# Long convolution of the first block: PE taps, norm and silu by tokens

## The reference, cut to what matters

```python
ya = a_val * jax.nn.sigmoid(a_gate)                      # 256 tokens x 512 channels
ya = causal_dwconv(ya, w_dw_a[l], b_dw_a[l])             # 31 taps, one weight per channel and tap
ya = jax.nn.silu(layer_norm(ya, ln_a_g[l], ln_a_b[l]))   # mean and variance over the 512 channels of a token
ya = ya @ w_pw_a[l]                                      # 512 -> 1024
...
merged = jax.nn.sigmoid(gate_a) * ya + jax.nn.sigmoid(gate_b) * yb
mix = merged @ w_out[l]
```

## Time and profile before

| | us |
|---|---|
| median of 3 runs | 1148.27 |
| lowest and highest | 1147.22, 1149.77 |
| the profiled execution, its own time | 1147.8 |
| its span in the profile | 1145.8 |
| busy: PE, PE weight loads | 1088.8, 1021.4 |
| busy: DVE, ACT, POOL | 798.3, 597.4, 3.3 |

### The profile page before, as it was taken

How to read it: one execution, slowest core, us unless ns; L and a number is a source line. 1 busy time by engine, 2 the same in 40 slices (tenths; PEclk the granted TensorE clock), 3 DMA queues, 4 the chain that set the end, 5 groups by cost and what they waited for, 6 DMA issues and landing times.

```text
span 1145.8 us, 19024 instructions
## 1 busy us (share of the span) xinstructions
PE 1088.8 (95%) x7792; PEld 1021.4 (89%) x7792; DVE 798.3 (70%) x1375; ACT 597.4 (52%) x1004; POOL 3.3 (0%) x13
## 2 busy tenths in 40 slices
PE   7998989999999999979989999999999899999997
PEld 7998879899999988779988799999899787999996
DVE  7988779878887778696664755555688747455555
ACT  5567444455556547642453644454565546444453
POOL 0000000000000000000000000000000000000000
PEclk9999989999999999989989999999999999999999
DMA  9985247257666624234222455556555335555520
GB/s 374 418 332 173 92 148 287 90 172 254 226 220 203 203 73 131 63 103 148 75 74 93 153 170 192 187 183 199 168 184 168 109 110 190 188 190 182 190 73 37
DMA packets 58549, 195.55 MB, mean 171 GB/s; under 512 B 10848, under 2 KB 11232, under 8 KB 58208
## 3 DMA queue, kind: packets, MB, share of 16 engines
q1 hardware_dynamic: 58464, 194.35, 50.0%
HBM read 193.01 MB, written 1.31 MB: 170 GB/s over the span
## 4 chain that ended last, share of the span: by engine, by line
PE 73%; DVE 18%; ACT 6%; issue 2%; SPq 1%; DMA 0%; POOL 0%; ACTq 0%; DVEq 0%; POOLq 0%
PE ps L542 61%; DVE lo L1644 5%; PE ps L816 3%; ACT hi L1119 2%; DVE raw L1631 2%; PE ps L699 1%; PE ps L644 1%; DVE B L2040 1%; DVE ev L1876 1%; PE ps L537 1%; DVE ev L1873 1%; PE ps L549 1%; DVE B L1653 1%; PE ps L822 1%; DVE B L1759 1%
## 5 line engine op out<-in xcount | busy, mean ns | idle before, releaser
L1644 DVE TENSOR_TENSOR lo<-raw,hi 128x1024 fp32r<-128x1024 f32 x311 | 377.3, 1222 | 163.3 <-ACT hi L1119 162.6
L542 PE MATMUL ps<-hh,hi 128*128 128x256 f32 x1568 | 448.4, 286 | 13.8 <-DVE hl L1736 3.2
L542 PE MATMUL ps<-hl,hi 128*128 128x256 f32 x1568 | 442.3, 282 | 0.0
L542 PE MATMUL ps<-hh,lo 128*128 128x256 f32 x1568 | 442.1, 282 | 0.0
L1119 ACT ACTIVATE hi<-raw 128x1024 fp32r<-128x1024 f32 x311 | 323.0, 1051 | 59.8 <-PE ps L542 59.8
L542 PEld LDWEIGHTS ps<-hh,hi 128*128 128x128 f32 x1568 | 298.9, 191 | 19.0 <-issue 9.1
L542 PEld LDWEIGHTS ps<-hl,hi 128*128 128x128 f32 x1568 | 299.1, 191 | 1.9
L542 PEld LDWEIGHTS ps<-hh,lo 128*128 128x128 f32 x1568 | 299.0, 191 | 0.0
L1350 ACT ACTIVATE ev<-ps 128x256 f32<-128x256 f32 x72 | 27.7, 385 | 109.6 <-PE ps L542 109.6
L542 PE MATMUL ps<-hi,fh 128*128 128x512 f32 x192 | 76.3, 398 | 0.0
L542 PE MATMUL ps<-lo,fh 128*128 128x512 f32 x192 | 75.9, 395 | 0.0
(11 more groups left out here) (274 smaller groups left out, 1325.3 us busy)
## 6 DMA issues: line engine op xcount, KB each, us to landing
raw<-in_w SPq DMA_DIRECT2D x359, 512.0 KB, 4.4
B<-in_t SPq DMA_DIRECT2D x2, 512.0 KB, 4.8
xa<-in_x SPq DMA_DIRECT2D x1, 1024.0 KB, 11.2
B<-in_r SPq DMA_DIRECT2D x1, 1024.0 KB, 7.7
out<-h SPq DMA_DIRECT2D x4, 256.0 KB, 2.0
cst<-in_c SPq DMA_DIRECT2D x1, 928.0 KB, 9.2
B<-between SPq DMA_DIRECT2D x32, 4.0 KB, 1.6
vec<-in_v SPq DMA_DIRECT2D x1, 328.5 KB, 7.3
```

The costliest lines, as they stand in the source:

```text
L542: m = g.matmul(o, l, r, start=first and n == 0, stop=last and n == 2, skip_group_check=True)
L1644: g.tensor_tensor(lo[:, j % SPLIT, :], raw[:, PLACE[j] % RAW, :], hi[:, j % SPLIT, :].bitcast(F), ALU.subtract).then_inc(*up("lo", j))
```

## The change

On TensorE a tap's operands change places: the window of `ypad` is the stationary operand, in two halves of 128 tokens, and the diagonal the moving one, so the sum comes out by tokens, bank 0 for the first 128 tokens and bank 1 for the others. VectorE's taps are added to it by matmuls with the identity. The norm is by tokens (bn_stats, bn_aggr, root, reciprocal), half on VectorE, half on ScalarE, into `yt` (in `B[2]`); the result is turned by transposes into banks 6 and 7, and silu reads these with gain and bias as its scale and bias. Silu's table is loaded ahead of ScalarE's half of the norm. The 52 filler matmuls of the norm become 16.

```diff
+        yt = B[2][:, :, :].rearrange("p a b -> p (a b)").rearrange("p (c n) -> p c n", c=2)
...
-            def spin(n):
+            def spin(n, b=7):
...
-                    g.matmul(bank[7][:, 0:S], idle[:, 0:P], idle[:, :], start=True, stop=True, skip_group_check=True)
+                    g.matmul(bank[b][:, 0:S], idle[:, 0:P], idle[:, :], start=True, stop=True, skip_group_check=True)
...
-                    s.wait_ge(*at("ya", t))
-                    g.matmul(acc(0, t), cv[:, 4 + (n_diag[0] % 8) // 2, (n_diag[0] % 2) * P:(n_diag[0] % 2) * P + P],
-                             ypad[:, t, 2 + i:2 + i + S], start=i == PE_TAPS[0] and t % 2 == 0, stop=i == 30,
-                             skip_group_check=True).then_inc(*up("conv", (i, t)))
+                    s.wait_ge(*at("ya", max(t, 1)))
+                    d = cv[:, 4 + (n_diag[0] % 8) // 2, (n_diag[0] % 2) * P:(n_diag[0] % 2) * P + P]
+                    for c in range(2):
+                        v = 2 + i + c * P
+                        m = g.matmul(bank[c][:, t * P:t * P + P], ypad[:, t, v:v + P], d, start=i == PE_TAPS[0] and t == 0,
+                                     stop=False, skip_group_check=True)
+                    m.then_inc(*up("conv", (i, t)))
...
-            norm("ya", cv, lambda k: at("conv_sum", 1), 4, 1, B[3], 0, 1)
+            for c in range(2):
+                for t in range(4):
+                    s.wait_ge(*at("tap", (PE_TAPS[0] - 1, t)))
+                    m = g.matmul(bank[c][:, t * P:t * P + P], cv[:, t, c * P:c * P + P], ident, start=False, stop=True,
+                                 skip_group_check=True)
+                m.then_inc(*up("ya_tok", c))
+            s.wait_ge(*at("yb", 7))
+            spin(10)
+            for c in range(2):
+                s.wait_ge(*(at("norm_a", ("ya", 1)) if c else at("norm_v", ("ya", 0))))
+                for t in range(4):
+                    a = (t % 2) * S + c * P
+                    m = g.transpose(bank[6 + t // 2][:, a:a + P], yt[:, c, t * P:t * P + P], ident)
+                m.then_inc(*up("turned", ("ya", c)))
+            s.wait_ge(*at("gate_b", 7))
+            spin(6, 5)
...
-                        [at("rstd", "ya")] if k == 0 else [])
+                        [at("silu_y", 3)] if k == 0 else [])
...
-            norm("ya", B[3], B[2], 1, 4)
-            norm_out("ya", 4, B[2], veccol("ln_a_g"), veccol("ln_a_b"), B[2])
+            for c in range(2):
+                s.wait_ge(*at("tmv", ("ya", c)))
+                g.activation(frs[:, c, :], fmv[:, c, 1:2], ACT.Sqrt, bias=eps[:, 0:1]).then_inc(*up("tsd", ("ya", c)))
+            table(ACT.Silu)
+            s.wait_ge(*at("tnm", ("ya", 1)))
+            g.activation(yt[:, 1, 0:512], bank[1][:, :], ACT.Identity, scale=frs[:, 1, :],
+                         bias=fnm[:, 1, :]).then_inc(*up("norm_a", ("ya", 1)))
+            s.wait_ge(*at("turned", ("ya", 1)))
             for k in range(4):
-                s.wait_ge(*(at("n_a", ("ya", k)) if k % 2 else at("n_v", ("ya", k))))
-                g.activation(cv[:, k, :], B[2][:, k, :], ACT.Silu).then_inc(*up("silu_y", k))
+                g.activation(cv[:, k, :], acc(6, k), ACT.Silu, scale=V("ln_a_g", k), bias=V("ln_a_b", k)).then_inc(*up("silu_y", k))
...
-            for b in range(2):
-                s.wait_ge(*at("conv", (30, 3)))
-                s.wait_ge(*at("tap", (14, 3)))
-                g.tensor_tensor(cv[:, 2 * b:2 * b + 2, :], cv[:, 2 * b:2 * b + 2, :], pair(b),
-                                ALU.add).then_inc(*up("conv_sum", b))
-
-
-            center("ya", cv, 4, B[3], B[2], 0)
-            root("ya")
-            norm_out("ya", 4, B[2], veccol("ln_a_g"), veccol("ln_a_b"), B[2])
+
+
+            for c in range(2):
+                s.wait_ge(*at("ya_tok", c))
+                g.bn_stats(fst[:, c, 0:6], bank[c][:, :]).then_inc(*up("tbn", ("ya", c)))
+                s.wait_ge(*at("tbn", ("ya", c)))
+                g.bn_aggr(fmv[:, c, :], fst[:, c, 0:6].rearrange("p (i n) -> p i n", i=1)).then_inc(*up("tmv", ("ya", c)))
+            for c in range(2):
+                s.wait_ge(*at("tsd", ("ya", c)))
+                g.reciprocal(frs[:, c, :], frs[:, c, :]).then_inc(*up("trs", ("ya", c)))
+                s.wait_ge(*at("trs", ("ya", c)))
+                if c == 0:
+                    g.tensor_scalar(yt[:, 0, 0:512], bank[0][:, :], fmv[:, 0, 0:1], frs[:, 0, :], ALU.subtract,
+                                    ALU.mult).then_inc(*up("norm_v", ("ya", 0)))
+                else:
+                    g.scalar_tensor_tensor(out=fnm[:, 1, :], in0=fmv[:, 1, 0:1], scalar=-1.0, in1=frs[:, 1, :], op0=ALU.mult,
+                                           op1=ALU.mult).then_inc(*up("tnm", ("ya", 1)))
```

## The result

| | before | changed |
|---|---|---|
| median, us | 1148.28 (4 runs, 1147.22 to 1149.77) | 1139.91 (4 runs, 1137.92 to 1140.03) |
| ratio | | 0.9922, 95% interval 0.9905 to 0.9939 |
| profiled execution, its span | 1147.8, 1145.8 | 1137.92, 1136.0 |

The change makes the kernel faster, by 8.4 us between the medians and by 9.0 by the ratio; 6.0 were forecast. Two later sets of runs gave the same code ratios of 0.9939 and 0.9952, that is 7.0 and 5.5 us, so the first measurement was the luckiest of three. Why it varies is a large part of what follows.

What follows compares the result with a forecast made beforehand. TensorE, busy 95%, bounds the kernel; 14.16 us between taps and `pw` could be won. Summed steps move `pw` from 147.08 to 141.15, 5.93 us less: 1142.3, own range 1141.3 to 1143.5, whole range 1139.5 to 1145.3.

Steps and rivals of the forecast that it cites:

- Taps by tokens: TensorE's taps: 16 records of 0.112 us each, nine taps on the chain 0.58 us longer, the other seven covered by waiting.
- the rival of slow weights: TensorE's taps: weights from `ypad` load slowly, 0.216 us per record, some 18 us slower, 1166; chance 0.05.
- Sum, statistics, root, transposes: Between taps and silu: identity matmuls 1.79 us, norm by tokens ending about 138.82, second transposes readable at 139.65.
- The table load: ScalarE's half of the norm: silu's load of 1.28 us stands ahead of it on the path, moved forward from silu's place.
- The rule that adds a drain to the load: ScalarE's half of the norm: a 1380 ns drain per table switch would cut the gain to 4.55 us; not adopted.
- Silu with scale and bias: Silu reading PSUM ahead of `pw`: 0.55 us, ending at 140.22, then 0.93 for split and TensorE's start.
- A shift as one piece: Stages behind `pw`: the same stages, each 6 us earlier, as both kernels reach `pw` with a full weight ring.
- The clock at `pw`: Start of `pw`: TensorE's clock falls to half again, as the idle pieces total 2.6 us; 1.7 us stays lost.
- my first rival: Start of `pw`: TensorE's clock stays up, 1.7 us more won, gain 7.6 us, 1140.6; chance 0.28.
- The clock in all other stages: Stages other than `pw`: no clock gain was counted, only a possible 1.7 us loss in a stage behind.
- a loss of that size behind the change: A stage behind that kept its clock before loses 1.7 us: gain 4.2 us, 1144.0; chance 0.13.
- the lower end of 1139.5: Bottom of the whole range, in us: the kept clock less 1.0 for a silu and a start at their shortest.

Runs made afterwards that it cites:

- e5: Changed kernel with both halves of the norm on VectorE, ScalarE's identity and the negated mean removed: ratio 0.9906, median 1138.4 us, norm 6.80 us.
- e6: Changed kernel without the table load ahead of ScalarE's half, so that it stands before the first silu: ratio 0.9944, median 1141.9 us, norm 7.52 us.
- e4: Changed kernel itself, unaltered, timed again with a second profile: ratio 0.9939, median 1140.8 us.
- e7: Changed kernel with 22 fillers between the `pw` and `out` matmuls: ratio 0.9958, median 1143.4 us.
- e11: Changed kernel itself, unaltered, timed a third time: ratio 0.9952, median 1142.6 us.
- e1: Kernel before with 22 more filler matmuls ahead of the first `pw` matmul: ratio 0.9981, median 1146.2 us.
- e3: Changed kernel with 37 fillers in its norm in place of 16: ratio 0.9941, median 1140.0 us.
- e8: Changed kernel with both norm halves on VectorE, 16, 4 and 12 fillers through the norm and 22 ahead of `out`: ratio 0.9921, median 1139.0 us.
- e9: Kernel before with 22 more fillers ahead of `pw`, timed in a second set: ratio 0.9981, median 1145.0 us.
- e10: Changed kernel with 37 fillers in its norm, timed in a second set: ratio 0.9926, median 1138.6 us.
- e12: Changed kernel with both norm halves on VectorE and 16, 4 and 12 fillers through the norm, none ahead of `out`: ratio 0.9917, median 1138.0 us.

## Why the prediction was off, point by point

**Taps by tokens: right.** Forecast plus 0.58, measured plus 0.54. Sixteen records take 1.78 us against 1.73 for eight of twice the width, 0.111 each, with the window of `ypad` as the weights; the rival of slow weights is gone. The seven earlier taps cost nothing: the changed kernel is 0.28 us ahead before them and 0.28 ahead behind them, and TensorE's wait for the pool result shrank from 2.47 to 2.35 us.

**Sum, statistics, root, transposes: right.** Every step has the duration of its row within 0.1 us. Forecast from last tap to `pw`: 7.65; measured 7.49. The largest deviations are the wait and the four transposes, from the end of ScalarE's half to silu's start (0.73 in place of 0.83), and ScalarE's half (0.68 in place of 0.75).

**The table load: right place, wrong reading of what it buys.** It was on the path (e5), but it would not have been longer in its old place (e6). The rule that adds a drain to the load, from the Trainium skill's page "ScalarE: Activation LUTs", section "What ACT_TABLE_LOAD costs", does not hold here: the chain goes on 0.01 us behind it (137.54, 137.56) and at 139.42 in e6. The same page of the Trainium skill, section "Table sets: the hidden batching unit", has identity in every set, and the trace agrees: the identity under silu's table at 137.76 made no load, and neither did silu behind it at 139.17.

**Silu with scale and bias: right.** 0.57 against 0.55; split and start 0.93 as before.

**A shift as one piece: right** up to the clock: 7.96 at `out` and 7.97 at 208 us, 8.7 at 430, 9.8 at the end.

**The clock at `pw`: this step failed.** I wrote that the idle pieces "add up to as much" as before and took the clock to fall again. The idle time before `pw` was not one piece of 2.83 us but pieces of 0.7, 1.0 and 0.8 with work between, and in six profiles with these 16 fillers (the changed one, e4, e5, e6, e7, e11) the clock was up at `pw` in three and half in three. (The pieces are 0.7, 0.3 and 0.8 in e5 and 0.7, 0.4 and 1.4 in e6; of the four with the changed kernel's own pieces, two have it up and two half.) Where it was up, 1.54 us came on top of 6.13; I had priced it at 1.7. With more fillers (e1, e3, e8, e9, e10, e12) it was up in six of six, which is few to compare. In other words, the change turned a loss that the only profile of the unfilled kernel before shows into a loss in every second execution, as far as six profiles tell. Whether the unfilled kernel before has that loss in every execution isn't shown. That the clock stays up was my first rival, with 0.28 and 1140.6; the measured 1139.9 is its case, with 0.7 us more that nothing in the sum accounts for.

**The clock in all other stages: a gain put at nothing.** 6.13 plus 1.54 is 7.7; the first measurement had 8.4 to 9.0, the later two 7.0 and 5.5. I gave the kept clock one step of 1.7, and to the other stages only a loss of that size behind the change; a gain from their clock, ahead or behind, I put at nothing without a reason, and so the lower end of 1139.5 was too high: the first ratio gives 1139.3 (0.9922 of 1148.28). The profiled pair has 9.8 us from span to span: 7.7, then 0.3 won ahead of the change and 1.8 behind it. The pool stage, which kept its clock in the profile of the earlier trace rows, lost it in four of the fourteen, and the end of the taps moves by 3.8 us between profiles of code that is the same up to there. So a part of the first measurement's 9.0 is luck, and the three sets together, 5.5 to 9.0, are the fairer answer. For the medians this isn't shown, since only one execution of each run has a profile.

## What to carry to other kernels

Where a norm over channels stands between two stretches of TensorE, have TensorE sum by tokens, take bn_stats straight from the bank, and transpose back: the roots and reciprocals shrink from 256 columns to one, and 14.2 us became 7.5, or 6.8 with VectorE doing both halves. Price such a rewrite from the chain, and write TensorE's clock down as a term of its own with both outcomes, for every stage that has idle time ahead of it and not only for the changed one. Here 1.5 us hung on it at `pw`, and fillers in the idle time kept it up in six profiles of six. Two profiles of the changed kernel differ by 4.8 us and by nothing in the norm, so compare stage by stage, from an instruction that both share. If a table load is on ScalarE's way, try first to give the work behind it to another engine: that won 0.7 us here, and moving the load won nothing.

## What the runs showed of the hardware that I had not expected

The same instruction sequence had its clock at half or at full in the same place from one execution to the next (8.66 or 10.2 us for 72 matmuls), with idle pieces of at most 1.0 us ahead of it. In the pool stage the clock was full behind 2.47 us of idle time and half behind 2.35. Fillers worth 2.6 us of TensorE's idle time brought the kernel before to a ratio of 0.9981, though they compute nothing. A table load placed before an activation began before that activation's inputs were ready (138.13 in e6, beside the transposes that end at 138.82). Four transposes at half rate took 1.13 us against 0.67. And keeping the clock up in one stage (e7, `out`) did not keep it up in the next: it fell in the norm behind.
